# The FFN result of tiles 0 and 1: only copied out of PSUM beside the last gathers, its norm and residual behind them

## The reference, cut to what matters

```python
u = expert_down[idx]; v = expert_up[idx]
act = gelu(einsum("td,thkd->thk", xb, u))
x = x + einsum("thk,thkd->td", gate * act, v)      # then the final rms norm
```

```python
h = modulate(rms_norm(x, norm_g[2]), sh_f, sc_f)
y = swiglu_ffn(h, ffn_w_in, ffn_w_out)
x = x + gt_f * rms_norm(y, norm_g[3])              # the step that the change moves, for tokens 0 to 255
```

## Time and profile before

| | us |
|---|---|
| median of 3 runs | 2212.55 |
| lowest and highest | 2205.64, 2213.81 |
| span of the profiled execution (no other time of it is given) | 2215.5 |
| PE busy | 1750.4 (79%) |
| DVE busy | 1328.7 (60%) |
| ACT busy | 896.0 (40%) |
| POOL busy | 846.6 (38%) |
| gather queue, share of 16 DMA engines over the span | 59.5% |

### The profile page before, as it was taken

The page is one execution under the profiler, slowest core; times in us unless marked ns, Lnnn a source line. Parts: engine busy times, 40 slices in busy tenths (PEclk is TensorE's granted clock), DMA queues, the critical chain, the costliest instruction groups (busy, mean ns, idle before and its releaser), DMA issues.

```text
span 2215.5 us, 26080 instructions
## 1 busy us (share of the span) xinstructions
PE 1750.4 (79%) x9120; PEld 1115.8 (50%) x9120; DVE 1328.7 (60%) x2912; ACT 896.0 (40%) x2387; POOL 846.6 (38%) x679
## 2 busy tenths in 40 slices
PE   7888887755667778855877775888888799968998
PEld 6784654413324525611344422455554348757997
DVE  4687558988788766566466666755555512324442
ACT  3111344443344434455455645423222334444443
POOL 0300243456566343444434343443333300034554
PEclk9998997867887898967989887999999889979999
DMA  7266699999999999999999999999999952123543
GB/s 281 86 242 233 250 418 408 408 376 368 377 350 419 417 417 418 418 416 417 367 418 418 418 419 419 416 418 419 419 419 419 391 196 84 59 87 113 189 188 114
DMA packets 115698, 726.10 MB, mean 328 GB/s; under 512 B 13168, under 2 KB 14192, under 8 KB 44400
## 3 DMA queue, kind: packets, MB, share of 16 engines
q0 software_dynamic: 73728, 536.90, 59.5%
q1 hardware_dynamic: 41840, 187.54, 22.3%
HBM read 720.20 MB, written 2.10 MB: 326 GB/s over the span
## 4 chain that ended last, share of the span: by engine, by line
PE 44%; DMA 23%; DVE 15%; issue 6%; ACT 6%; POOL 5%; SPq 0%; DVEq 0%; POOLq 0%; PEldq 0%; ACTq 0%
PE ps L923 44%; DMA arena<-in_experts,arena_u 22%; DVE arena L2453 6%; POOL arena L2089 3%; ACT arena L1763 1%; DVE arena L2146 1%; ACT sel L1759 1%; DVE arena L2294 1%; ACT L1759 0%; DVE selu L2166 0%; ACT L1607 0%; DVE arena L2149 0%; POOL r_high L2116 0%; DMA middle<-in_w_late 0%; DVE arena L2293 0%
## 5 line engine op out<-in xcount | busy, mean ns | idle before, releaser
L923 PE MATMUL ps<-arena 128*128 128x256 f32 (+4 forms) x6088 | 1301.8, 519 | 337.6 <-ACT arena L1763 294.3
L923 PEld LDWEIGHTS ps<-arena 128*128 128x128 f32 (+2 forms) x6088 | 757.3, 175 | 841.5 <-ACT arena L1763 389.8
L2089 POOL DMA_INDIRECT arena<-in_experts,arena_u x512 | 588.8, 1150 | 842.7 <-PE ps L923 753.1
L2453 DVE CUSTOM_DVE_ANT_0 arena<-arena 128x1024 f32<-128x1024 f32 x512 | 644.9, 1265 | 402.5 <-DMA arena<-in_experts,arena_u 394.4
L1759 ACT ACTIVATE sel<-sel 128x1 f32<-128x1 f32 x512 | 102.7, 201 | 713.6 <-DVE sel L2453 707.0
L2116 POOL TENSOR_TENSOR r_low<-middle,r_low 128x1024 fp32r<-128x1024 f32 x48 | 122.1, 2549 | 262.7 <-ACT r_low L1913 262.7
L1763 ACT ACTIVATE arena<-arena,sel 128x32 f32<-128x32 f32 x512 | 164.5, 321 | 16.8 <-issue 0.2
L923 PE MATMUL ps<-r_low 128*128 128x256 f32 (+1 forms) x1104 | 139.5, 289 | 7.1 <-DVE r_low L2527 6.1
L923 PEld LDWEIGHTS ps<-r_low 128*128 128x128 f32 x1104 | 137.0, 194 | 9.6 <-issue 6.4
L923 PE MATMUL ps<-arena,consts 128*32 128x512 f32 (+5 forms) x672 | 97.7, 487 | 53.7 <-POOL arena L2070 29.9
L1752 ACT ACTIVATE arena<-consts,arena 128x32 f32<-128x32 f32 x512 | 120.7, 308 | 0.0
(11 more groups left out here) (247 smaller groups left out, 1504.0 us busy)
## 6 DMA issues: line engine op xcount, KB each, us to landing
arena<-in_w_front SPq DMA_DIRECT2D x88, 512.0 KB, 4.0
middle<-in_w_late SPq DMA_DIRECT2D x18, 2048.0 KB, 8.0
arena<-in_w_ada SPq DMA_DIRECT2D x48, 512.0 KB, 5.0
arena<-in_w_qkv SPq DMA_DIRECT2D x48, 512.0 KB, 6.9
arena<-in_w_late SPq DMA_DIRECT2D x22, 1024.0 KB, 13.1
arena<-in_w_late SPq DMA_DIRECT2D x30, 512.0 KB, 7.9
arena<-in_experts,arena_u POOLq DMA_INDIRECT x512
x<-in_x SPq DMA_DIRECT2D x4, 512.0 KB, 8.8
```

Of the source, the lines that this page charges most:

```text
L923: return nc.tensor.matmul(out_, lhsT, rhs, start=start, stop=stop_, skip_group_check=skip)
L2089: nc.gpsimd.indirect_dma_start(ring[n % RING], None, a["experts"], bass.IndirectOffsetOnAxis(ap=idxq[:, i % 4, k:k + 1], axis=0),).then_in ...
L2453: nc.vector.tensor_tensor_reduce(r[:, 0:D], r[:, 0:D], xrep[k % 4], 1.0, 0.0, ALU.mult, ALU.add, dots[:, n % 8:n % 8 + 1]).then_inc(s["dot ...
```

## The change

ScalarE's and VectorE's stages "br" 1 are gone from the plan. At load 501 ScalarE does a new stage "yo": it copies the FFN rows of both tiles out of PSUM into two buffers (`y_keep`) and raises `yfree`. TensorE's transposes of tile 2 wait for `yfree` and no longer for `fin`. Squares, square root, norm and residual are made from `y_keep` behind the gather: on ScalarE after tile 3's modulation and the constants, on VectorE after tile 3's norm. SP gets a wait for `fin` before the first late weight, since its buffer overlaps `y_keep`. Counts of `yfree` rise by two where they are waited for later.

```diff
@@ half_plan
-    act.append((FFN_END + 4, "br", 1))
-    dve.append((FFN_END + 5, "br", 1))
+    act.append((FFN_END + 4, "yo", 0))
@@ buffers
+        y_keep = [region(kb, D) for kb in (48, 52)]
@@ SP, first late weight
                     sp.wait_ge(s["seln"], T)
+                    sp.wait_ge(s["fin"], 2)
@@ TensorE, tile_transposes
                 elif t == 2:
-                    pe.wait_ge(s["fin"], 2)
+                    pe.wait_ge(s["yfree"], 4)
@@ ScalarE, half_stage
+                elif stage == "yo":
+                    sc.wait_ge(s["used"], h_used("fo", FT - 1))
+                    for t in range(2):
+                        nc.scalar.activation(y_keep[t], ps[:, 2 * t:2 * t + 2, :].rearrange("p b n -> p (b n)"), ACT.Copy).then_inc(s["yfree"], 1)
@@ ScalarE, behind the gather, after the four constants
+            sc.wait_ge(s["yfree"], 4)
+            for t in range(2):
+                nc.scalar.activation(region(80 + 4 * t, D), y_keep[t], ACT.Square, accum_out=stat[:, 8, t:t + 1]).then_inc(s["ysq"], 1)
+            sc.wait_ge(s["ysq"], 8)
+            nc.scalar.activation(stat[:, 9, 0:2], stat[:, 8, 0:2], ACT.Sqrt, bias=EPS, scale=1.0 / D).then_inc(s["ysq"], 1)
             nc.scalar.preload_act_table_set("natural_log_exp_and_others")
@@ VectorE, behind the gather, after tile_norm(T - 1, 1)
+            ve.wait_ge(s["ysq"], 9)
+            own.step(nc.vector.reciprocal(stat[:, 9, 0:2], stat[:, 9, 0:2]))
+            for t in range(2):
+                own.step(stt(y_keep[t], y_keep[t], stat[:, 9, t:t + 1], gtrow[:, 1, :], ALU.mult, ALU.mult))
+                tt(x[:, t, :], x[:, t, :], y_keep[t], ALU.add).then_inc(s["fin"], 1)
```

More of the change, by code:

```diff
@@ L1560, in rows_after @@
             def rows_after(t):
-                pe.wait_ge(s["yfree"], 2 + t + 1)
+                pe.wait_ge(s["yfree"], 4 + t + 1)
                 pe.wait_ge(s["xs"], T + 2 + t + 1)
@@ L1786, in tile_modulate @@
                                          bias=modc[:, 0, kd:kd + 1], scale=stat_mod(0, kd)).then_inc(s["a_y"], 1)
-            h_junk = [[region(152, D), region(156, D)], [region(64, D), region(68, D)]]
+            h_junk = [region(152, D), region(156, D)]
             def half_stage(stage, arg):
@@ L1824, in half_stage @@
                     nc.scalar.activation(qA[:, i, :], ps[:, 2 * (i % 2), 0:SH], ACT.Copy).then_inc(s["o_hi"], 1)
+                elif stage == "yo":
+                    sc.wait_ge(s["used"], h_used("fo", FT - 1))
+                    for t in range(2):
+                        nc.scalar.activation(y_keep[t], ps[:, 2 * t:2 * t + 2, :].rearrange("p b n -> p (b n)"), ACT.Copy).then_inc(s["yfree"], 1)
                 elif stage == "br":
                     k = arg
-                    sc.wait_ge(s["used"], h_used("ow", KD - 1) if k == 0 else h_used("fo", FT - 1))
+                    sc.wait_ge(s["used"], h_used("ow", KD - 1))
                     for t in range(2):
-                        nc.scalar.activation(h_junk[k][t], ps[:, 2 * t:2 * t + 2, :].rearrange("p b n -> p (b n)"), ACT.Square,
+                        nc.scalar.activation(h_junk[t], ps[:, 2 * t:2 * t + 2, :].rearrange("p b n -> p (b n)"), ACT.Square,
                                              accum_out=stat[:, 8, t:t + 1]).then_inc(s["ysq"], 1)
-                    sc.wait_ge(s["ysq"], 6 * k + 2)
+                    sc.wait_ge(s["ysq"], 2)
                     nc.scalar.activation(stat[:, 9, 0:2], stat[:, 8, 0:2], ACT.Sqrt, bias=EPS, scale=1.0 / D).then_inc(s["ysq"], 1)
@@ L1836, in half_stage @@
                         sc.wait_ge(s["yfree"], t + 1)
-                        nc.scalar.activation(h_junk[0][t], x[:, t, :], ACT.Square, accum_out=stat[:, 10, t:t + 1]).then_inc(s["ysq"], 1)
+                        nc.scalar.activation(h_junk[t], x[:, t, :], ACT.Square, accum_out=stat[:, 10, t:t + 1]).then_inc(s["ysq"], 1)
                     sc.wait_ge(s["ysq"], 5)
@@ L1966, in stats_after @@
             def stats_after(t):
-                sc.wait_ge(s["yfree"], 2 + t + 1)
+                sc.wait_ge(s["yfree"], 4 + t + 1)
                 sc.wait_ge(s["ssq"], 4 * T + 2 * t)
@@ L2413, in half_stage @@
                 elif stage == "br":
-                    k = arg
-                    ve.wait_ge(s["ysq"], 6 * k + 3)
+                    ve.wait_ge(s["ysq"], 3)
                     own.step(nc.vector.reciprocal(stat[:, 9, 0:2], stat[:, 9, 0:2]))
@@ L2418, in half_stage @@
                         y = ps[:, 2 * t:2 * t + 2, :].rearrange("p b n -> p (b n)")
-                        own.step(stt(h_dst[t], y, stat[:, 9, t:t + 1], gtrow[:, k, :], ALU.mult, ALU.mult))
-                        tt(x[:, t, :], x[:, t, :], h_dst[t], ALU.add).then_inc(s["yfree" if k == 0 else "fin"], 1)
+                        own.step(stt(h_dst[t], y, stat[:, 9, t:t + 1], gtrow[:, 0, :], ALU.mult, ALU.mult))
+                        tt(x[:, t, :], x[:, t, :], h_dst[t], ALU.add).then_inc(s["yfree"], 1)
                 elif stage == "sa":
```

## The result

| kernel | median us | runs | ratio to the kernel before, 95% interval |
|---|---|---|---|
| before | 2211.91 (2203.41 to 2216.16) | 20 | |
| after | 2214.28 (2210.03 to 2219.01) | 20 | 1.002 [1.0011, 1.0029] |
| after, second session | 2211.98 (before there: 2210.78) | 12 | 1.0014 [1.0, 1.0028] |

The change makes the kernel slower by 0.2%: 2.4 to 6.4 us by the interval. That is inside the 0.5% forecast as "no change", and on the side of the +1.2 us of the sum, but the interval begins only where the forecast's band of -0.5 to +2.5 us ends.

What follows compares the result with a forecast made beforehand. The prediction took the gather's DMA queue, not VectorE's 5.2 us, as the bound: -1.04 (landing gap) + 2.2 (shared DMA) + 0 (moved work) + 0 (clock) = +1.2 us, 2213.7 us against the median, range 2205 to 2222.

Steps and rivals of the forecast that it cites:

- the sum: Whole kernel: -1.04 us from the gather's landings, +2.2 from shared DMA, 0 for moved work, 0 for TensorE's clock: +1.2 us.
- the forecast's band: Whole kernel: a time change of -0.5 to +2.5 us, 2212 to 2215 us, given a chance of 0.60.
- The 5.2 us on the chain: Near the gather's end: VectorE's FFN norm and residual leave the chain of waits, but the DMA queue behind them still bounds.
- The issue comes 5.2 us earlier: Last gathers: loads 510 and 511 are issued 5.2 us earlier, as are the sums before SP's value loads.
- The hole: Gather's landings: the 3.54 us gap before load 510 closes to 2.50, so the last dot product starts 1.04 us earlier.
- Sharing costs 2.2 us: End of the gather: SP's earlier value loads share the DMA engines with the last gathers; 1.9 to 3.0 us, taken as 2.2.
- The rule of turns packet by packet: DMA engines at the gather's end: equal turns between queues would give late loads half the engines, net +3.2 us.
- The moved work is hidden: Behind the gather: ScalarE's added 2.7 us and VectorE's 5.2 us fit in idle times of 8.74 and 41.51 us; cost 0.
- TensorE's clock: Tail's start on TensorE: the clock level may change, -3.2 us at best, +0.9 at worst; taken as 0.
- Sharing does not bite: Rival at the gather's end: value loads come too late or gather goes first; -1.0 to -4.2 us, chance 0.19.
- all 5.2 us: Rival: all of VectorE's time taken off the chain of waits is won, 2207.3 us; chance 0.06.
- crowded out: Rival at the gather's end: 4.2 MB of value loads enter before loads 509 to 511 finish; net +3.2 to +9 us, chance 0.15.

Runs made afterwards that it cites:

- before_tailwork: Kernel before, with the moved ScalarE and VectorE work added a second time behind the gather, on scratch buffers: 0.9993 [0.9979, 1.0006] of the kernel before.
- before_hold: Kernel before, with SP's eight value loads held until the sums of loads 508 and 509 are done: 1.0002 [0.9986, 1.0017] of the kernel before.
- hold: Changed kernel, with SP's eight value loads held until the sums of loads 508 and 509 are done: 0.9993 [0.9979, 1.0007] of the kernel before.
- warm: Changed kernel, with unused TensorE products added behind the sums of loads 506 to 509 (5, then 6): 1.0016 [1.0003, 1.0029] of the kernel before.
- hold_half: Changed kernel, with only the last four of SP's eight value loads held until the sums of 508 and 509: 1.0025 [1.0012, 1.0037] of the kernel before.
- hold_warm: Changed kernel, with all eight value loads held and fewer unused TensorE products added (2, then 3): 0.9992 [0.998, 1.0005] of the kernel before.
- before_3: Kernel before, unchanged, third profile: one run without a ratio, 78.83 us from the dot product of load 501 to the attention's scores.

## Why the prediction held, and where it was off

- *The 5.2 us on the chain are not the bound.* Right. They left the chain, and the last gather landed no earlier.
- *The issue comes 5.2 us earlier.* Right, 5.9 for load 511 by the ruler's start; 4.5 for the value loads.
- *The hole is worth 1.04 us.* Over-sized. It was one profile's: the last two intervals of the kernel before are 6.03, 5.37 and 5.68 us in three, 0.7 us over 4.98 in the mean. With the same late issue they are 5.37 in before_tailwork and 5.01 in before_hold, so what the late issue costs varies from nothing to 1.04 us, and why is open.
- *Sharing costs 2.2 us.* Right: 6.62, 7.27 and 6.78 less 4.98 are 1.6, 2.3 and 1.8 us, and hold takes them away. That the value loads were harmless before is right too: the gather's last packets are 0.31 us apart there. What was not foreseen is that at the end one late engine decides, and that the cost goes by its packets: 0.47 us instead of 0.31 for each, half as much again. The 0.46 to 0.72 taken from the stretch at 1700 lies close to that, though it was read from another mixture of loads, which is in part luck. The rule of turns packet by packet (the Trainium skill, DMA: Bandwidth & Descriptors, "Queues, rings and completion order") agrees with this trace, one value packet between two gather packets. The 4.2 us that the prediction made of it counted a turn of either queue as equally long; here a value packet's turn lasts 0.16 us and a gather packet's 0.31.
- *The moved work is hidden.* Right: 6.44 us of idle time left, and before_tailwork.
- *TensorE's clock, taken as 0, with +0.9 as its worst.* This is the term that was mis-sized. From the last dot product to the scores it is 50.6 us where the clock stays high (51.8 in warm, whose added products ran over), 53.1 to 53.5 where it is low, so the clock is worth some 2.5 to 3 us there. After the change it is low in three profiles of three (and in hold_half): 53.34, 53.55, 53.28. Before it is 53.08, 50.57, 53.20: the one profile that I worked from had the low clock already, so it showed what could be won and hid what could be lost. In the mean it is +1.1 us (+1.5 with before_tailwork as a fourth profile of the code before). It is a loss apart from the sharing: with the value loads held the clock is low in three profiles of three as well. The cause in the clock's case is shown in part: added work ahead of the last sums brings the high level back (warm, hold_warm). That the idle time of 5.35 us is the reason is argued, and the rows do not bear it out: with held loads the sums are at the low level behind 3.0 to 3.9 us of idle time, in before_3 behind 2.05 us, and in the first profile of before they are at the high level behind 2.34 us.
- *The sum.* On the ruler the mean of three profiles is 78.02 us before and 80.39 after, +2.4: +1.3 up to the last dot product (forecast: +1.2) and +1.1 behind it (forecast: 0). The first agrees partly by luck: the hole (0.7 for 1.04) and the sharing (1.9 for 2.2) were both taken 0.3 us too large, with opposite signs. With before_tailwork as a fourth profile the ruler before is 77.5 us, and the difference +2.9. The measured +2.4 to +6.4 includes it at its edge; in the second session it is 0 to +6.2. What more there may be lies outside this stretch, and single profiles, 9 us apart ahead of it, can't show it. The times of hold and hold_warm (2207.70 and 2207.59, 12 runs each) show nothing of the 2.7 us between their rulers, but each ratio's interval is 3 us wide on either side, so they do not speak against it.
- *The rivals.* "Sharing does not bite" falls by the intervals, "all 5.2 us" by the landings, "crowded out" in its size for the gather's end: value data do take turns with the last packets, but for 1.9 us in the mean, not for 4.2 to 10.

## What to carry to other kernels

When a stall is on the chain, look at what it holds back besides the work on the chain: here, transfers in another queue that were harmless only because they were late. A buffer that comes free earlier is a reason to bind its refill to the end of the stream that it would disturb, as hold did with one wait. What the disturbance costs is counted in the packets that the disturbed stream still has on its latest engine, not in the bytes queued beside it. And before a term is taken from one profile of a kernel whose runs spread, take a second profile: the hole and the clock level differed between executions of the same program.

## What was not expected of the hardware

The last landings of the gather hang on a single file of packets: 6.2% of the 16 engines is busy, an 8 KB packet starts every 0.31 us, or every 0.47 us once another queue has data, and the last interval goes from 2.49 to 3.79 us with it. The clock of TensorE differed between executions of the same program at the same place, last sums of 1.06 and 1.87 us in the kernel before, and so did the 1744.2 to 1753.4 us ahead of it.
